# Turns of the blockwise inverse: products with the identity, or transposes where the turn lands in the lower partitions

## Time and profile before

| | us |
|---|---|
| median of 3 runs | 3290.6 (3290.12 to 3290.84) |
| profiled execution, its own time | 3288.91 |
| its span | 3287.1 |

### The profile page before, as it was taken

One profiled execution on the slowest core, in us unless ns is written; L12 is line 12 of the kernel. 1 busy time (PEld: TensorE's weight loads), 2 busy tenths in 40 slices (PEclk: granted clock), 3 DMA queues, 4 the chain that ended last, 5 costly groups with the idle time before them and its releaser, 6 DMA issues. The chain is left out here.

```text
span 3287.1 us, 56382 instructions
## 1 busy us (share of the span) xinstructions
PE 3210.5 (98%) x23386; PEld 2744.4 (83%) x23386; DVE 1654.8 (50%) x2484; ACT 1286.7 (39%) x2064; POOL 62.5 (2%) x79
## 2 busy tenths in 40 slices
PE   8999999999999999999998999999999999999999
PEld 7997889889788988888887888788888888876899
DVE  7744574774457552223674667542233323247444
ACT  5433454544345452223543444432223222234433
POOL 0000000000000010000000000000000000000000
PEclk9999999999999999999999999999999999999999
DMA  6545654454655432222221333222222222211353
GB/s 260 180 167 220 227 189 169 180 179 157 253 205 180 178 116 102 93 99 90 103 78 64 131 118 131 79 103 90 102 90 90 90 102 90 102 64 39 129 180 127
DMA packets 62918, 439.27 MB, mean 134 GB/s; under 512 B 6672, under 2 KB 9872, under 8 KB 10000
## 3 DMA queue, kind: packets, MB, share of 16 engines
q1 hardware_dynamic: 61552, 435.43, 36.7%
q10 hardware_dynamic: 1184, 1.18, 0.1%
HBM read 435.54 MB, written 1.05 MB: 133 GB/s over the span
## 5 line engine op out<-in xcount | busy, mean ns | idle before, releaser
L701 ACT ACTIVATE sb_w_split<-sb_ring 128x2048 fp32r<-128x2048 f32 x263 | 504.2, 1917 | 905.4 <-PE ps_low L465 706.0
L709 DVE TENSOR_TENSOR sb_w_split<-sb_ring,sb_w_split 128x2048 fp32r<-128x2048 f32 x263 | 603.3, 2294 | 432.3 <-ACT sb_w_split L701 432.3
L465 PE MATMUL ps_low<-sb_x_split,sb_w_split 128*128 128x512 f32 (+1 forms) x3520 | 691.3, 355 | 18.6 <-DVE sb_w_split L735 13.4
L465 PE MATMUL ps_high<-sb_x_split,sb_w_split 128*128 128x512 f32 (+1 forms) x3520 | 685.2, 353 | 1.9 <-DVE sb_w_split L709 1.9
L465 PEld LDWEIGHTS ps_low<-sb_x_split,sb_w_split 128*128 128x128 f32 x3520 | 579.5, 189 | 119.6 <-DVE sb_w_split L735 13.4
L465 PEld LDWEIGHTS ps_high<-sb_x_split,sb_w_split 128*128 128x128 f32 x3520 | 580.1, 189 | 96.8 <-DVE sb_w_split L709 2.9
L465 PE MATMUL ps_low<-sb_a_split,sb_w_split 128*128 128x256 f32 (+1 forms) x2112 | 370.2, 325 | 0.0
L465 PE MATMUL ps_high<-sb_a_split,sb_w_split 128*128 128x256 f32 (+1 forms) x2112 | 368.2, 323 | 0.0
L465 PEld LDWEIGHTS ps_low<-sb_a_split,sb_w_split 128*128 128x128 f32 x2112 | 314.2, 190 | 37.6 <-DVE sb_w_split L709 2.8
L465 PEld LDWEIGHTS ps_high<-sb_a_split,sb_w_split 128*128 128x128 f32 x2112 | 314.2, 190 | 30.4
L465 PE MATMUL ps_low<-sb_xn,sb_ring 128*128 128x256 f32 (+1 forms) x800 | 184.3, 388 | 0.5 <-ACT sb_xn L2652 0.5
(11 more groups left out here) (376 smaller groups left out, 3181.0 us busy)
## 6 DMA issues: line engine op xcount, KB each, us to landing
sb_ring<-weights SPq DMA_DIRECT2D x411, 1024.0 KB, 4.8
sb_consts<-consts SPq DMA_DIRECT2D x1, 2020.0 KB, 14.9
sb_h<-xT SPq DMA_DIRECT2D x1, 1024.0 KB, 6.9
sb_h<-ctxT ACTq DMA_DIRECT2D x1, 1024.0 KB, 20.8
out<-sb_h SPq DMA_DIRECT2D x1, 1024.0 KB, 4.8
sb_vectors<-vectors SPq DMA_DIRECT2D x1, 269.0 KB, 2.9
sb_arena<-positions ACTq DMA_DIRECT2D x1, 128.0 KB, 7.1
```

The source lines that it names most:

```text
L465: ins = self.g.nc.tensor.matmul(out, lhsT, rhs, start=start, stop=stop)
L701: g.nc.scalar.activation(g.w_split[:, 0, s % 2, :], g.ring[:, n % SLOTS, :], ACT.Copy).then_inc(g.sem["w_high"], 1)
L709: g.nc.vector.tensor_tensor(g.w_split[:, 1, s % 2, :], g.ring[:, n % SLOTS, :], g.w_split[:, 0, s % 2, :].bitcast(F32), ALU.subtract).then ...
```

## The change

A new helper, `turn`, makes a turn as `nc.tensor.transpose` with the same identity if its output lies in the lower partitions, and as the product it was otherwise. All turns of the inverse go through it: the start's, the levels' (where what counts is the half in which the block lands), the tail's. Of the 96 turns of a step 48 become transposes: 8 of 16 in the start, 8 of 16 in each of four levels, 8 of 16 in the tail. The order of all work, the tiles and the semaphores stay.

```diff
+    def turn(self, out, in_, rows, to, full=None):
+
+        side = self.g.const("block_identity")[rows, :]
+        if to == LOW_HALF:
+            ins = self.g.nc.tensor.transpose(out, in_, side)
+        else:
+            ins = self.g.nc.tensor.matmul(out, lhsT=in_, rhs=side, start=True, stop=True)
+        if full:
+            ins.then_inc(self.g.sem[full + "_full"], 1)
+        elif self.unreleased:
             ins.then_inc(self.unreleased.pop(0), 1)
...
# start_transposes
-                pe.mm(tile[rows, block(h)], b["turned"][rows, d, block(h)], g.const("block_identity")[rows, :],
-                      full="low" if h == GH - 1 and rows == HIGH_HALF else None)
+                pe.turn(tile[rows, block(h)], b["turned"][rows, d, block(h)], rows, rows,
+                        full="low" if h == GH - 1 and rows == HIGH_HALF else None)
...
# both_transposes
-                    pe.mm(tiles[d][landing(rows, d), block(h)], b["inv"][rows, d, block(h)], g.const("block_identity")[rows, :],
-                          full="low" if h == GH - 1 and rows == HIGH_HALF else None)
+                    pe.turn(tiles[d][landing(rows, d), block(h)], b["inv"][rows, d, block(h)], rows, landing(rows, d),
+                            full="low" if h == GH - 1 and rows == HIGH_HALF else None)
...
# the tail, direction 0 beside the corners
-                pe.mm(turns[0][rows, block(h)], b["inv"][rows, 0, block(h)], g.const("block_identity")[rows, :])
+                pe.turn(turns[0][rows, block(h)], b["inv"][rows, 0, block(h)], rows, rows)
...
# the tail, the rest
-                pe.mm(turns[d][rows, block(h)], b["inv"][rows, d, block(h)], g.const("block_identity")[rows, :],
-                      full="low" if h == GH - 1 and rows == HIGH_HALF else None)
+                pe.turn(turns[d][rows, block(h)], b["inv"][rows, d, block(h)], rows, rows,
+                        full="low" if h == GH - 1 and rows == HIGH_HALF else None)
```

More of the change, by code:

```diff
@@ L465, in mm @@
         ins = self.g.nc.tensor.matmul(out, lhsT, rhs, start=start, stop=stop)
+        if full:
+            ins.then_inc(self.g.sem[full + "_full"], 1)
+        elif self.unreleased:
+            ins.then_inc(self.unreleased.pop(0), 1)
+    def turn(self, out, in_, rows, to, full=None):
[4 more added lines that the diff above has]
+            ins = self.g.nc.tensor.matmul(out, lhsT=in_, rhs=side, start=True, stop=True)
         if full:
```

## The result

| | before | after |
|---|---|---|
| median of the runs, us | 3290.36 (4 runs, 3285.47 to 3290.84) | 3378.64 (4 runs, 3377.93 to 3382.08) |
| profiled execution, its own time | 3288.91 | 3377.93 |
| its span | 3287.1 | 3376.1 |

The ratio is 1.028 (95% interval 1.0268 to 1.0292): the change makes the kernel about 88 us slower. The forecast was 3364 in a range of 3284 to 3400.

What follows compares the result with a forecast made beforehand. The prediction took the turns, in a ring of waits between TensorE, ScalarE and VectorE, as the bound. Longer turns of 78 to 92 us, less cover, gave 66 to 80, taken as 73: 3364 us, range 3284 to 3400.

Steps and rivals of the forecast that it cites:

- Where the turns stand: Eight-step stage of 297.60 us: the turn is on the path, since the copy after it waits for it.
- the ring of waits: In the stage, VectorE waited 52.6 us for TensorE's high tiles, ScalarE 40.9 and 36.0 for its low tiles.
- The transposes save nothing by themselves: All turns: low turns fall from 0.117 to about 0.058 us, but high turns beside them stay; 0 us, down to -7.
- A small fp32 transpose stands at full width: In the turns, a narrow fp32 transpose holds the array's full width of columns, so changing to 64x64 products costs time.
- Quarters side by side, 0.058 us an instruction: Turns: four array quarters work at once in levels, two in the start; each needs about 0.058 us per instruction.
- a passage empties the array: Each change between transposes and 64x64 products in the turns drains TensorE, 0.09 to 0.12 us; this forecast case had 62%.
- Price of a segment: Runs of one turn kind: products 0.256 us, transposes 0.149 to 0.198; 9.8 to 11.5 a step, 78 to 92 in eight.
- What covers some: Levels' earlier tile handover and the tail's ScalarE copies hide 8 us in all; 4 us of issue waits also go.
- of 12.2 us of issue I let 4 go: TensorE's unexplained waits in the stage: a slower TensorE asks for instructions more slowly, so 4 of 12.2 us vanish.
- The clock: If TensorE's granted clock, 0.97 in the stage, falls in emptier stretches, more; a further tenth at half level is 15 us.
- side by side: Rival, 22%: in the turns, transposes run beside products in the 64x64 layout; 0 us, 3287 to 3293, level still 0.52.
- in order without emptying: Rival, 8%: in the turns, transpose and product can't overlap but nothing is drained; +17 us, 3307, level 0.8.

Runs made afterwards that it cites:

- The grouped run: Changed kernel with each set's low-landing turns first, then the high-landing ones (tail: corners and high turns first); ratio 1.0021 to the kernel before, +7 us.
- the constants' run: Kernel before plus 59 small transposes and products on constants in TensorE's 8 us wait ahead of the first step; 3280.81 us against 3280.57.
- the padded run: Kernel before plus three products of constants ahead of the turns in each of the 32 levels, no transposes; ratio 1.0083, +27 us.
- the bench: Kernel before plus 59 small instructions on constants ahead of the first step, the same run as the constants' run; 3280.81 us against 3280.57.

## Why the prediction was right or wrong

- *Where the turns stand.* Right: the ring of waits grew with the turns, nothing outside the stage moved, and ScalarE's longer wait (47 us) is in the 40 to 60 named. The stage foreseen at some 370 us up to the end used there is 377 up to the end used here; it took 391.9.
- *The transposes save nothing by themselves.* Right in kind: half the instructions of a low turn went, and the high turns set the end. The grouped run shows what the forecast did not see, that the freed low quarters can start the next products.
- *A small fp32 transpose stands at full width.* Read from transposes of 128 rows and 4 columns that paid no passage; the constants' run agrees at 64 rows: 0.28 us a pair beside the 64x128 product, which is the instructions' own time, and 0.43 beside the quarter product in place of the 0.117 of two rounds. This was the step that decided, and it held. That a passage empties the array was my reading and is not shown; the traces show only the time, 0.15 us from the last start before a passage to the next (1800.54 to 1800.68) where the starts before it are 0.056 apart.
- *Quarters side by side, 0.058 us an instruction.* Every segment's price was built on this, and the starts in the trace of before bear it out. The level's 32 turns, from 2014.63 on, come four at a time: 8 have started by 2014.77, 12 by 2014.83, 16 by 2014.89, 20 by 2014.95. The start's, from 1998.93 on, come two at a time: 4 by 1999.05, 6 by 1999.11, 8 by 1999.17. Both are 0.058 us apart. The 0.05 of a first round also goes with late loads there: the turns' loads and the turns both start at 2014.63, the loads of the products behind them at 2015.09, 0.06 ahead of the products.

```profile
2014.63 0.40 PE L465 MATMUL ps_low<-sb_consts,sb_xn 64*64 64x64 f32 x12
2014.63 0.46 PE L465 MATMUL ps_low<-sb_consts,sb_xn 64*64 64x64 f32 x16
1998.93 0.39 PE L465 MATMUL ps_low<-sb_consts,sb_xn 64*64 64x64 f32 x6
1998.93 0.45 PE L465 MATMUL ps_low<-sb_consts,sb_xn 64*64 64x64 f32 x8
2015.09 0.21 PEld L465 LDWEIGHTS ps_low<-sb_xn 64*64 64x64 f32 x8
```

- *Price of a segment.* Products 0.256, measured 0.26; transposes 0.149 to 0.198, measured 0.17 to 0.18. Start 3.42 us (foreseen 3.24 to 3.63), level 1.92 (1.77 to 2.01), tail 3.72 (3.50 to 3.89), each read as the usual one of the eight or 32. Together (3.42 - 1.08) x 8 + 1.40 x 32 + (3.72 - 1.09) x 8 = 84.6 us, in the 78 to 92.
- *What covers some.* Too small. The prediction gave 8 us to the copies and 4 to the waits called "issue", 12 in all. All cover is time in which TensorE would have been idle, and that fell by 19.4 - 1.7 = 17.7 us, 6 more than foreseen. The term that was too small is "of 12.2 us of issue I let 4 go": all 12.2 went, and the 4.0 us for ScalarE too. The run with transposes in the levels alone shows the same; the padded run, without a transpose, shows it for the 4.0 us and for 8.0 of the 12.2. The reason given for the 4, that a slower TensorE asks for instructions more slowly, was my guess: no run shows a rate of asking, only these waits.
- *The clock.* Named ("more"), but put at nothing in the sum, and this is the larger miss. The clock records of both traces hold two levels, 1.00 and 0.50 (before, 0.50 from 1805.5 to 1815.0 and 1.00 from 1816.0 to 1900.0); after:

```profile
1870.00:1907.00 37.00, 36.92 (x603) 30.94 (x602) 23.64 (x68) 14.79 (x41) 0.00 (x0) 1.00 0.17 59
1909.00:1934.00 25.00, 25.00 (x347) 20.28 (x349) 7.31 (x21) 7.32 (x19) 0.00 (x0) 0.50 0.25 86
```

  With these, 0.97 over 304.0 us and 0.90 over 391.9 are some 18 and 78 us at the lower level, 60 more. The prediction tied a loss to emptier stretches; the stage lost this clock with 1.7 us of idle time in place of 19.4. TensorE's busy time rose by 390.2 - 284.6 = 105.6 us, of which the turns at full clock are 84.6. The 21.0 left over are 0.35 us for each of the 60. The level from 1915.63, at 0.50, agrees: 0.93 us lost in 2.85, or 0.33.

The account of the two traces: 84.6 for the longer turns, 21.0 for the rest of TensorE's busy time, which goes with the lower clock, less 17.7 of idle time taken back, is the 87.9 measured. The 21.0 is a difference, not a measurement of its own, and these are single traces: that of the bench, whose eight steps are those of the kernel before, has a stage of 296.9 us with 15.6 of idle time and 6.4 of "issue" where the trace of before has 304.0, 19.4 and 12.2. The forecast of +73 missed +88 by 15 only because two errors stood against each other: no clock, by 21, and too little cover, by 6. Of the rivals, side by side and in order without emptying are excluded by 1.92 us where they wanted 0.52 and 0.8.

## What to carry to other kernels

Here a cheaper instruction cost far more than it saved: 0.43 us a pair beside products with which it pays a passage, 0.28 beside longer ones with which it does not. So look for a row in which its kind stands between products of the size it will have as neighbours, and count passages, not instructions. If both are needed, group them: the same 384 transposes cost 88 us alternating and 7 grouped. And before adding up a delay of the busiest engine, take the waits that it will no longer have (17.7 us here), those called "issue" included.

## What was not expected of the hardware

- Lost clock came with alternation in the start and the tail: the stage's granted clock was 0.93 and 0.95 with one of these alone, 0.99 with the levels alone. The third step of the changed kernel ran at a mean of 0.74. Why these, and why that step, is open.
- TensorE's waits called "issue", 12.2 us in the stage of before in pieces of up to 1.7 us, were gone when TensorE had 1.4 us more in each level, and stayed in part when the time was added as padding (4.2 us), in the start (9.4) or in the tail (8.2). They also differ from trace to trace, as the bench's 6.4 us show.
- Quarters run ahead of each other: with the low quarters free, products started at 2018.44 in the grouped run, 0.17 us before the last turn ahead of them in the program (2018.61).
